# Twelve taps of a depthwise convolution move from the latents to behind the first eight softmax maxima and into the attention loop

## The chip, the cores and the metric

One core of a Trainium2 chip runs the whole program in one launch. The metric is the device time in microseconds (us). Before the change it is 3565.58 us, the median of three runs (3564.41 to 3566.22).

## The reference

Three transformer-like layers are computed one after the other on a sequence of 1024 positions and 1024 channels, in fp32. Only the second layer matters here. Cut to the part around the change:

```python
def hybrid_layer(h, ...):
    z = rms_norm(h, mix_norm_g) @ w_in
    a, gate, c_q, c_kv, k_r = jnp.split(z, ...)          # 512, 512, 384, 256, 32 columns
    u = a * jax.nn.sigmoid(gate)
    u = causal_depthwise_conv(u, conv_w, conv_b)         # 31 taps on 512 channels
    u = jax.nn.silu(layer_norm_2(u, conv_ln_g, conv_ln_b))
    q  = rms_norm(c_q, q_norm_g) @ w_uq                  # 8 heads of 64 + 32 (rotated)
    kv = rms_norm(c_kv, kv_norm_g) @ w_ukv
    ...
    o = block_causal_attention(qf, kf, v, chunk_id)      # softmax(q k) v, 8 heads
    mix = jnp.concatenate([rms_norm(u, conv_out_g), rms_norm(o, attn_out_g)], axis=-1)
    h = h + mix @ w_out
    ...
```

The convolution of u (31 taps, 4 blocks of 128 channels) does not depend on the attention, and the attention does not depend on it. Both must be there before the product with w_out.

## The kernel before, in words

The program is written out by hand, one list of instructions for each engine, with semaphores between them. Activations lie transposed: channels on the 128 partitions, the positions (1024, or 1044 with meta tokens and padding in layer 2) along the row. A product with weights is three matmuls, high part by high part and two cross terms (`product`, L253, its matmuls L270 to L272; `product_by_piece` L339 and `three` L320 with L324 to L326; `moving_product` L358 with L374 to L376). Weights come in tiles of eight 128x128 blocks: SyncE loads `w_raw`, ScalarE rounds it to `w_hi` (L131), GpSimd makes `w_lo` (L98 on POOL).

Layer 2's mixer is the class `Mixer2` (L1435). Its stages, in the order of the work:

- **The latents.** TensorE makes fourteen products from the input, each 8 blocks by 3 pieces of 348 columns: gate 0 and a 0, gate 1 and a 1, c 3, c 4, rot, then a sum over squares, c 0, c 1, c 2, another sum, gate 2, a 2, gate 3, a 3. A product takes three PSUM banks, and there are two such sets, so that each product waits until VectorE has read the last but one before it. VectorE reads them in `dve_gate` (L2088), `dve_row` (L2125), `dve_rotate_keys` (L2142) and `dve_normed` (L2137).
- **The heads' start.** Values (`pe_values`, L1693), the first keys and the first queries, which wait for five rows that VectorE writes to `x_lo` at the end of `dve`'s latents.
- **The first eight scores.** Before the attention loop TensorE computes the eight score tiles of head 0 (`pe_score`, L1741), and VectorE takes the maximum of each (`dve_max`, L2187, two TENSOR_REDUCE of line L113 each, and at some a small minimum), from which the softmax's shift comes. The score tiles lie in two places in PSUM, so that score n waits for the maximum n-2; the rows of shifts (`pe_row`, L1764) wait for the fifth and the eighth maximum, and the attention's first chunks wait for those rows.
- **The attention loop.** 160 slots, 20 for each of the 8 heads (`for c in range(len(CHUNKS2))`). In the slots 8 to 15 of a head the next head's eight scores and maxima are made in the same way, and in the slots before them its keys and queries.

The convolution is a side branch, a generator for each engine (`pe_branch`, `act_branch`, `dve_branch`, L1516 to L1616). The first 124 steps of VectorE's generator are the taps: one pass over a row of 1044 elements each, a TENSOR_SCALAR (L104) for the first tap of a block of channels and SCALAR_TENSOR_TENSOR (L107, `mix<-u_padded,vectors,mix`) for the other thirty. The layer norm of the result follows in 28 further steps, with sums on TensorE and squares, roots and the silu on ScalarE. `advance(branch, n)` issues n steps at that place of the engine's queue. A table of numbers says where:

```python
TAPS = dict(gate=[(0, 0), (1, 5), (1, 5), (1, 5)], a=(5, 5, 5, 0), row=(4, 5, 4, 5, 5), rot=2, kv=1, q=2)
STEPS, LAST_STEP = 91, 140
done = [min(x, self.LAST_STEP) * self.STEPS // self.LAST_STEP for x in (c, c + 1)]
```

`gate[c]` holds the taps before and after the second multiplication in `dve_gate`; `a[c]` those behind gate and product c; `row[i]` those behind row i (the rows go in the order 3, 4, 0, 1, 2); `rot`, `kv` and `q` those behind the rotation and the two normings. That is 61 in the latents. In the loop, slot c issues as many steps as its share of `STEPS` over 140 slots says (`taps`, L1511): 91 steps, of which 63 are the remaining taps. The generators of TensorE and ScalarE skip as many steps ahead of the loop (`early_taps`, L1506), so that the three stay in step.

Of the kernel before, what the change touches and what calls it, by code (L numbers as in the profile page):

```python
# [145 lines left out]
def advance(steps, n):  # L146

    for _ in range(n):
        if next(steps, None) is None:
            return  # L150


def drain(steps):
    for _ in steps:
        pass
# [10 lines left out]
def thirds_of(t):  # L166
    return t.rearrange("p (a b) -> p a b", a=3)
# [1267 lines left out]
class Mixer2:  # L1435
# [6 lines left out]

    TAPS = dict(gate=[(0, 0), (1, 5), (1, 5), (1, 5)], a=(5, 5, 5, 0), row=(4, 5, 4, 5, 5), rot=2, kv=1, q=2)
    ROUND_AT = 6
    SCORE_AT = {8: 3, 9: 8, 10: 2, 11: 7, 12: 1, 13: 6, 14: 4, 15: 5}
    ROW_AT = {15: (0,), 18: (1, 2)}
    SMALL = (0, 4, 8)
    STEPS, LAST_STEP = 91, 140  # L1450

    def __init__(self, core, ffn):
        self.k, self.ffn, s = core, ffn, core.s
# [51 lines left out]

    def early_taps(self):  # L1506

        return sum(sum(x) if isinstance(x, tuple) else x for x in (*self.TAPS["gate"], self.TAPS["a"], self.TAPS["row"], self.TAPS["rot"],
                                                                   self.TAPS["kv"], self.TAPS["q"]))

    def taps(self, c):  # L1511

# [575 lines left out]
    def dve_gate(self, v, c, branch):  # L2088
# [19 lines left out]
        else:  # L2108
            v.wait_ge(*p.done)
            v.settle()  # L2110
            v.tt(thirds_of(self.sig), k.view(p), thirds_of(self.rms), ALU.mult, inc=p)
        advance(branch, self.TAPS["gate"][c][0])
        v.wait_ge(self.gate_sig, c + 1)
        v.tt(self.sig, self.sig, self.rms, ALU.mult)
        advance(branch, self.TAPS["gate"][c][1])
        v.settle()
# [126 lines left out]
    def dve(self, v):  # L2243
        k = self.k
        branch = self.dve_branch(v)
        v.memset(self.u_pad[:, :, 0:CONV2 - 1], 0.0)
        for c in range(2):
            self.dve_gate(v, c, branch)
            advance(branch, self.TAPS["a"][c])
        for n, i in enumerate((3, 4)):  # L2250
            self.dve_row(v, i, n)
            advance(branch, self.TAPS["row"][i])
        self.dve_rotate_keys(v)
        advance(branch, self.TAPS["rot"])
        self.dve_normed(v, ("kv rms",), (3, 4), 2, "kv_norm_g_2")
        advance(branch, self.TAPS["kv"])
        for n, i in enumerate((0, 1, 2)):
            self.dve_row(v, i, n)
            advance(branch, self.TAPS["row"][i])
        self.dve_normed(v, ("q rms",), (0, 1, 2), 3, "q_norm_g_2")  # L2260
        advance(branch, self.TAPS["q"])
        for c in (2, 3):
            self.dve_gate(v, c, branch)
            advance(branch, self.TAPS["a"][c])
        for n, i in enumerate((3, 4, 0, 1, 2)):
            v.wait_ge(self.p_rounded, n + 1)
            v.tt(k.x_lo[:, i, :], self.T[i], k.x_hi[:, i, :].bitcast(F32), ALU.subtract, inc=self.p_ready)
        self.dve_heads(v)
        self.dve_at = [k.at["latents"][1]]
        self.dve_products(v, "heads")  # L2270
        for n in range(len(self.SCORE_AT)):
            self.dve_max(v, n)
        item = len(self.SCORE_AT)
        for c in range(len(CHUNKS2)):
            h, s = divmod(c, A_HEAD)
            self.dve_products(v, ("fill", c))
            if h + 1 < H2 and s in self.SCORE_AT:
                self.dve_max(v, item)
                item += 1
            advance(branch, self.taps(c))  # L2280
            if self.ended(c - 2) is not None:
                self.dve_inverse(v, self.ended(c - 2))
            if self.ended(c - 4) is not None:
                self.dve_head_out(v, self.ended(c - 4))
            if c >= self.LAST_STEP + 4 and c % 4 == 0:
                self.dve_u_row(v, (c - self.LAST_STEP) // 4 - 1)
        self.dve_inverse(v, 3 * H2 - 1)
        self.dve_head_out(v, 3 * H2 - 1)
        drain(branch)
        for c in range(4):  # L2290
            self.dve_o_row(v, c)
        for m in range(8):
            p, x = k.products["uo", m], k.res[:, m, :]
            v.wait_ge(*p.done)
            v.wait_ge(self.h0_back[m // 2], 48)
            v.tt(thirds_of(x), thirds_of(x), k.view(p), ALU.add, inc=p)
        self.dve_root(v, ("o rms",), self.A[0], self.A[1], 4, 4 * P)
        for m in range(8):
            p, x = k.products["oo", m], k.res[:, m, :]
            v.wait_ge(*p.done)  # L2300
            v.settle()
            v.tt(thirds_of(self.A[2]), k.view(p), thirds_of(self.A[0]), ALU.mult, inc=p)
            v.settle()
            v.tt(x, x, self.A[2], ALU.add, inc=self.added)
            v.wait_ge(self.h_square, m + 1)
            if m:
                v.settle()
                v.tt(self.T[8], self.T[8], self.T[9], ALU.add, inc=self.h_total)
            if m < 4:
                self.dve_out_row(v, m)  # L2310
        for m in range(4, 8):
            self.dve_out_row(v, m)
# [1171 lines left out]
```

## Time and profile before

| | before |
|---|---|
| median of 3 runs | 3565.58 us (3564.41 to 3566.22) |
| the profiled execution | 3567.81 us |
| its span on the core | 3565.7 us |
| mean granted TensorE clock | 0.978 |
| TensorE matmul busy | 3406.3 us (96%) |
| VectorE busy | 1775.1 us (50%) |
| ScalarE busy | 1118.9 us (31%) |
| GpSimd busy | 1085.4 us (30%) |
| stretch of the latents | about 1281 to 1445 us |
| first eight maxima | 1471.6 to 1481.1 us |
| attention loop | about 1482 to 1805 us |

In the rows below PE is TensorE, PEld its weight loads, DVE VectorE, ACT ScalarE, POOL GpSimd. A start is counted from the start of the span. What stands in square brackets behind an instruction is how long its engine sat idle before it, and whose instruction ended that; a short fall of the clock shows in the column PEclk, where 1.00 is the full level and 0.50 the half.

### The profile page before, as it was taken

What the parts mean: (1) busy time and instruction counts of PE and PEld (TensorE: products, weight loads), DVE (VectorE), ACT (ScalarE), POOL (GpSimd) and SP (SyncE); (2) the same over time, 40 slices, a digit from 0 to 9 for tenths busy, and PEclk for the clock granted to TensorE, in tenths of its full rate; (3) what the DMA queues carried; (4) which work ended last, traced back from release to release, by engine and by line L of the source; (5) the groups of instructions that cost most, each with busy time, mean ns of one, the idle gap of its engine ahead of it and who ended that gap; (6) DMA issues with size and microseconds to landing.
All of it is one profiled execution on the core that took longest, in us unless ns stands there. A gap on an engine that the chain in (4) does not pass through costs nothing.

```text
span 3565.7 us, 39250 instructions
## 1 busy us (share of the span) xinstructions
PE 3406.3 (96%) x16240; PEld 2787.2 (78%) x16240; DVE 1775.1 (50%) x1897; ACT 1118.9 (31%) x1493; POOL 1085.4 (30%) x1144
## 2 busy tenths in 40 slices
PE   8998899999999998899799999999999999999997
PEld 7665677888888688655489999999987788888776
DVE  4557553222223578777547546445475423444532
ACT  4333343111112432344533111111142523333442
POOL 3111344222333433100013434334334222222253
PEclk9999999999999999899899999999999999999998
DMA  3000221111111221000021111111112111010242
GB/s 126 24 24 24 101 71 60 53 48 48 48 48 49 76 84 40 26 7 7 6 76 45 42 54 42 48 49 47 48 42 107 54 65 53 30 36 31 82 142 95
DMA packets 56249, 192.21 MB, mean 54 GB/s; under 512 B 6900, under 2 KB 7284, under 8 KB 55560
## 3 DMA queue, kind: packets, MB, share of 16 engines
q1 hardware_dynamic: 56072, 189.71, 15.4%
q8 instruction: 128, 2.10, 0.2%
q14 instruction: 49, 0.40, 0.0%
HBM read 172.83 MB, written 16.86 MB: 53 GB/s over the span
## 4 chain that ended last, share of the span: by engine, by line
PE 80%; DVE 14%; ACT 4%; issue 1%; DMA 0%; POOL 0%; DVEq 0%; ACTq 0%; SPq 0%; POOLq 0%
PE psum L270 21%; PE psum L271 21%; PE psum L272 21%; PE psum L138 11%; DVE mix L107 3%; DVE work L98 3%; PE psum L324 2%; PE psum L326 2%; PE psum L325 2%; DVE res L98 1%; DVE res L107 1%; DVE softmax_shift_columns L113 1%; DVE u_padded L98 1%; PE psum L136 1%; DVE work L116 1%
## 5 line engine op out<-in xcount | busy, mean ns | idle before, releaser
L98 POOL TENSOR_TENSOR w_lo<-w_raw,w_hi 128x256 fp32r<-128x256 f32 x1140 | 1085.2, 983 | 2445.6 <-ACT w_hi L131 2445.6
L270 PE MATMUL psum<-x_hi,w_hi 128*128 128x512 f32 (+2 forms) x3240 | 1202.9, 371 | 12.6 <-DVE mix L98 5.9
L271 PE MATMUL psum<-x_lo,w_hi 128*128 128x512 f32 (+2 forms) x3240 | 1165.8, 360 | 0.0
L272 PE MATMUL psum<-x_hi,w_lo 128*128 128x512 f32 (+2 forms) x3240 | 1161.9, 359 | 0.0
L131 ACT CAST w_hi<-w_raw 128x1024 fp32r<-128x1024 f32 x285 | 298.2, 1048 | 1503.7 <-PE psum L272 1429.7
L270 PEld LDWEIGHTS psum<-x_hi,w_hi 128*128 128x128 f32 x3240 | 613.5, 189 | 101.7 <-issue 18.6
L271 PEld LDWEIGHTS psum<-x_lo,w_hi 128*128 128x128 f32 x3240 | 613.0, 189 | 82.9 <-issue 18.4
L272 PEld LDWEIGHTS psum<-x_hi,w_lo 128*128 128x128 f32 x3240 | 611.2, 189 | 70.2
L270 PE MATMUL psum<-h_hi,w_hi 128*128 128x512 f32 x824 | 325.2, 395 | 3.1 <-DVE res L98 3.1
L272 PE MATMUL psum<-h_hi,w_lo 128*128 128x512 f32 x824 | 320.8, 389 | 0.0
L271 PE MATMUL psum<-h_lo,w_hi 128*128 128x512 f32 x824 | 320.7, 389 | 0.0
L107 DVE SCALAR_TENSOR_TENSOR res<-res,psum 128x1024 f32<-128x1024 f32 (+1 forms) x88 | 90.3, 1026 | 238.6 <-PE psum L272 229.3
L270 PEld LDWEIGHTS psum<-h_hi,w_hi 128*128 128x128 f32 x824 | 154.7, 188 | 37.8 <-DVE res L98 3.5
L271 PEld LDWEIGHTS psum<-h_lo,w_hi 128*128 128x128 f32 x824 | 154.7, 188 | 34.2 <-issue 2.6
L272 PEld LDWEIGHTS psum<-h_hi,w_lo 128*128 128x128 f32 x824 | 154.6, 188 | 32.3
L138 PE MATMUL psum<-res 128*65 128x256 f32 (+5 forms) x480 | 172.7, 445 | 7.1 <-ACT res L131 4.2
L98 DVE TENSOR_TENSOR h_tmp<-h_tmp 128x1024 f32<-128x1024 f32 (+1 forms) x36 | 54.7, 1518 | 240.7 <-ACT h_tmp L126 240.7
L107 DVE SCALAR_TENSOR_TENSOR mix<-u_padded,vectors,mix 128x1044 f32<-128x1044 f32 x120 | 168.5, 1404 | 5.0 <-ACT work L131 0.8
L98 DVE TENSOR_TENSOR up<-psum,ffn_rms 128x1026 f32<-128x1026 f32 x44 | 54.0, 1226 | 191.1 <-PE psum L272 189.4
L324 PE MATMUL psum<-x_hi,w_hi 128*128 128x348 f32 (+2 forms) x328 | 130.1, 397 | 18.2 <-DVE x_lo L98 9.2
L107 DVE SCALAR_TENSOR_TENSOR up_conv<-up,vectors,up_conv 128x1024 f32<-128x1024 f32 x88 | 143.7, 1633 | 3.1
L98 DVE TENSOR_TENSOR res<-res,psum 128x1024 f32<-128x1024 f32 (+1 forms) x56 | 68.5, 1224 | 140.9 <-PE psum L272 135.8
(281 smaller groups left out, 3730.5 us busy)
## 6 DMA issues: line engine op xcount, KB each, us to landing
w_raw<-w_dram SPq DMA_DIRECT2D x285, 512.0 KB, 3.2
res<-spill SPq DMA_DIRECT2D x4, 1044.0 KB, 8.9
res<-x_dram SPq DMA_DIRECT2D x8, 512.0 KB, 9.0
res<-x_dram SPq DMA_DIRECT2D x4, 1024.0 KB, 8.1
spill<-res SPq DMA_DIRECT2D x1, 4096.0 KB, 13.8
spill_a<-mix SPq DMA_DIRECT2D x8, 512.0 KB, 2.9
res<-spill_a SPq DMA_DIRECT2D x8, 512.0 KB, 4.7
x_plain<-spill SPq DMA_DIRECT2D x4, 1024.0 KB, 9.4
```

The costliest lines, as they stand in the source:

```text
L98: self.mark(self.e.tensor_tensor(out, a, b, op), inc)
L107: self.mark(self.e.scalar_tensor_tensor(out, a, s, b, op0, op1), inc)
L113: self.mark(self.e.tensor_reduce(out, a, AX.X, op, negate=negate), inc)
L116: self.mark(self.e.reciprocal(out, a), inc)
L131: self.mark(self.e.copy(out, a), inc)
L138: ins = self.e.matmul(out, lhsT, rhs, start=start, stop=stop, skip_group_check=True)
L270: t.e.matmul(out, whi, xhi, start=k == 0, stop=False, skip_group_check=True)
L271: t.e.matmul(out, whi, xlo, start=False, stop=False, skip_group_check=True)
L272: ins = t.e.matmul(out, wlo, xhi, start=False, stop=last_k, skip_group_check=True)
L324: t.e.matmul(out, whi, xhi, start=first, stop=False, skip_group_check=True)
L325: t.e.matmul(out, whi, xlo, start=False, stop=False, skip_group_check=True)
L326: return t.e.matmul(out, wlo, xhi, start=False, stop=last, skip_group_check=True)
```

## The change

Twelve taps leave the latents: five behind row 4 (the taps just ahead of the rotation), three behind row 2, four behind gate and product 2. Eight of them go one behind each of the first eight maxima, ahead of the loop. The other four go to the loop, whose `STEPS` rise from 91 to 95. `early_taps` counts the eight, so that the other engines' generators start the loop at step 57 and not 61; the last step stays in slot 139.

```diff
-    TAPS = dict(gate=[(0, 0), (1, 5), (1, 5), (1, 5)], a=(5, 5, 5, 0), row=(4, 5, 4, 5, 5), rot=2, kv=1, q=2)
+    TAPS = dict(gate=[(0, 0), (1, 5), (1, 5), (1, 5)], a=(5, 5, 1, 0), row=(4, 5, 1, 5, 0), rot=2, kv=1, q=2)
...
-    STEPS, LAST_STEP = 91, 140
+    STEPS, LAST_STEP = 95, 140
...
     def early_taps(self):

-        return sum(sum(x) if isinstance(x, tuple) else x for x in (*self.TAPS["gate"], self.TAPS["a"], self.TAPS["row"], self.TAPS["rot"],
-                                                                   self.TAPS["kv"], self.TAPS["q"]))
+        return len(self.SCORE_AT) + sum(sum(x) if isinstance(x, tuple) else x for x in (
+            *self.TAPS["gate"], self.TAPS["a"], self.TAPS["row"], self.TAPS["rot"], self.TAPS["kv"], self.TAPS["q"]))
...
         for n in range(len(self.SCORE_AT)):
             self.dve_max(v, n)
+            advance(branch, 1)
```

By the table, the taps of each head's 20 slots (slots 0 to 7, 8 to 14, 15 to 19) were 5, 4 and 4 in every head, 13 in all. Now heads 0, 2 and 4 have 5, 5 and 3 (still four of them in slots 9 to 14, and one in slot 8), and heads 1 and 3 have 6, 4 and 4: in head 1 the slots 5, 6 and 7 have a tap each, where two of them had one, and in head 3 slot 0 has the added one. The last tap of all moves from slot 16 of head 4 to slot 18, and the steps of the layer norm behind it come one or two slots later, up to head 6.

VectorE's queue in the latents, behind row 4 of the products (`work<-work` adds the squares; `mix<-psum,mix` and `psum<-psum,mix` are the first two instructions of the rotation of the keys, which reads the product rot):

```order
 L98 TENSOR_TENSOR res<-psum,work 128x1044
 L98 TENSOR_TENSOR work<-work 128x1044
-L107 SCALAR_TENSOR_TENSOR mix<-u_padded,vectors,mix 128x1044 x5
 L98 TENSOR_TENSOR mix<-psum,mix 32x1044
 L98 TENSOR_TENSOR psum<-psum,mix 32x3x348
```

The five taps between row 4 and the rotation are gone; nothing else moved there.

VectorE's queue at the first maxima, before (each pair of TENSOR_REDUCE is one maximum):

```order
L98 TENSOR_TENSOR work<-work 32x348
L113 TENSOR_REDUCE softmax_shift_columns<-psum 128x1
L113 TENSOR_REDUCE own_chunk_shift<-psum 64x1
L113 TENSOR_REDUCE softmax_shift_columns<-psum 128x1
L113 TENSOR_REDUCE own_chunk_shift<-psum 64x1
L113 TENSOR_REDUCE softmax_shift_columns<-psum 128x1
L113 TENSOR_REDUCE own_chunk_shift<-psum 64x1
```

and now:

```order
L98 TENSOR_TENSOR work<-work 32x348
L113 TENSOR_REDUCE softmax_shift_columns<-psum 128x1
L113 TENSOR_REDUCE own_chunk_shift<-psum 64x1
L107 SCALAR_TENSOR_TENSOR mix<-u_padded,vectors,mix 128x1044
L113 TENSOR_REDUCE softmax_shift_columns<-psum 128x1
L113 TENSOR_REDUCE own_chunk_shift<-psum 64x1
L107 SCALAR_TENSOR_TENSOR mix<-u_padded,vectors,mix 128x1044
L113 TENSOR_REDUCE softmax_shift_columns<-psum 128x1
L113 TENSOR_REDUCE own_chunk_shift<-psum 64x1
L107 SCALAR_TENSOR_TENSOR mix<-u_padded,vectors,mix 128x1044
```

One tap stands behind every maximum, up to the eighth.

VectorE's queue at the end of the latents (`u_padded<-psum,work` ends product 2 and product 3 of a; the first `work<-psum,work` reads gate 3):

```order
 L98 TENSOR_TENSOR u_padded<-psum,work 128x1044
-L107 SCALAR_TENSOR_TENSOR mix<-u_padded,vectors,mix 128x1044 x5
+L107 SCALAR_TENSOR_TENSOR mix<-u_padded,vectors,mix 128x1044
 L98 TENSOR_TENSOR work<-psum,work 128x1044
 L107 SCALAR_TENSOR_TENSOR mix<-u_padded,vectors,mix 128x1044
```

Four of the five taps ahead of gate 3 are gone.

## Rows read from the trace of the kernel before

**Rows 1.** The page: the chain that ended last, shares by engine.

```profile
PE 80%; DVE 14%; ACT 4%; issue 1%; DMA 0%; POOL 0%; DVEq 0%; ACTq 0%; SPq 0%; POOLq 0%
```

**Rows 2.** Waits of PE in the latents and heads' start: us in total, times, longest.

```profile
PE psum L270 <- DVE mix L98: 5.3, 1, 5.3
PE psum L374 <- DVE x_lo L98: 3.9, 1, 3.9
...
PE psum L270 <- DVE work L98: 2.4, 1, 2.4
```

**Rows 3.** Timeline of DVE behind row 4: start, us, instruction, xcount, idle before.

```profile
1338.64 7.17 DVE L107 SCALAR_TENSOR_TENSOR mix<-u_padded,vectors,mix 128x1044 f32<-128x1044 f32 x5
1345.94 1.25 DVE L98 TENSOR_TENSOR mix<-psum,mix 32x1044 f32<-32x1044 f32 x1
```

**Rows 4.** Timelines of ACT and PE: the end of rot, the start of c 0.

```profile
1342.79 1.05 ACT L131 CAST w_hi<-w_raw 128x1024 fp32r<-128x1024 f32 x1 [5.46 <-PE psum L272]
...
1349.81 0.66 PE L270 MATMUL psum<-x_hi,w_hi 128*128 128x348 f32 x1 [5.35 <-DVE mix L98]
```

**Rows 5.** Windows: us, busy (x) of PE, PEld, DVE, ACT, POOL; PEclk, DMA share, GB/s.

```profile
1306.70:1312.00 5.30, 5.27 (x23) 5.28 (x24) 5.22 (x4) 2.02 (x2) 3.14 (x3) 0.68 0.27 99
...
1349.80:1355.00 5.20, 5.20 (x18) 5.20 (x19) 5.03 (x4) 0.00 (x0) 0.00 (x0) 0.50 0.11 44
1355.00:1361.00 6.00, 6.00 (x39) 6.00 (x38) 5.83 (x7) 0.00 (x0) 0.00 (x0) 1.00 0.00 0
```

**Rows 6.** Timeline of DVE: start of the norming of q, behind row 2.

```profile
1399.35 1.25 DVE L98 TENSOR_TENSOR work<-squares 128x1044 f32<-128x1044 f32 x1 [2.84 <-ACT squares L126]
```

**Rows 7.** Timelines of DVE and ACT at the end of the latents.

```profile
1430.62 1.25 DVE L98 TENSOR_TENSOR work<-psum,work 128x1044 f32<-128x1044 f32 x1
1443.17 7.08 DVE L98 TENSOR_TENSOR x_lo<-res,x_hi 128x1044 fp32r<-128x1044 f32 x5
...
1429.44 1.05 ACT L131 CAST w_hi<-w_raw 128x1024 fp32r<-128x1024 f32 x1 [10.35 <-PE psum L272]
1441.80 4.91 ACT L131 CAST x_hi<-res 128x1044 fp32r<-128x1044 f32 x5
```

**Rows 8.** The chain that ended last, in order of time, at the first maxima.

```profile
1473.94 1.14 PE psum L138 x2
...
1481.17 4.57 PE psum L138 x11
```

**Rows 9.** Timeline of DVE at the first maxima and behind them.

```profile
1471.61 0.51 DVE L113 TENSOR_REDUCE softmax_shift_columns<-psum 128x1 fp32r<-128x336 f32 x1 [1.95 <-PE psum L138]
...
1475.10 1.04 DVE L113 TENSOR_REDUCE softmax_shift_columns<-psum 128x1 fp32r<-128x848 f32 x1 [0.56 <-PE psum L138]
...
1477.52 0.91 DVE L113 TENSOR_REDUCE softmax_shift_columns<-psum 128x1 fp32r<-128x720 f32 x1 [0.15 <-PE psum L138]
...
1480.96 0.16 DVE L98 TENSOR_TENSOR softmax_shift_columns<-softmax_shift_columns 128x2 fp32r<-128x2 f32 x1
1488.35 0.52 DVE L98 TENSOR_TENSOR work<-psum,mix 64x348 f32<-64x348 f32 x1 [7.23 <-PE psum L326]
```

**Rows 10.** Windows of the first maxima and of the loop's start, columns as in rows 5.

```profile
1471.00:1482.00 11.00, 7.65 (x25) 4.71 (x26) 8.14 (x20) 0.79 (x2) 0.00 (x0) 0.50 0.00 0
1482.00:1502.00 20.00, 19.56 (x71) 11.48 (x70) 10.49 (x14) 9.70 (x24) 5.27 (x4) 0.85 0.02 3
```

**Rows 11.** Taps by tile (duration ns min/median/max), and POOL's one group on the page.

```profile
L107 DVE SCALAR_TENSOR_TENSOR mix<-u_padded,vectors,mix x120: 1304/1306/1807, 1298.6 to 1670.2; 128x1044 f32<-128x1044 f32 x120
...
L98 POOL TENSOR_TENSOR w_lo<-w_raw,w_hi 128x256 fp32r<-128x256 f32 x1140 | 1085.2, 983 | 2445.6 <-ACT w_hi L131 2445.6
```

**Rows 12.** Timeline of DVE in the attention loop: next head's second maximum, slack behind the eighth.

```profile
1544.23 1.16 DVE L113 TENSOR_REDUCE softmax_shift_columns<-psum 128x1 fp32r<-128x960 f32 x1 [0.90 <-PE psum L138]
...
1684.80 0.52 DVE L98 TENSOR_TENSOR work<-psum,mix 64x348 f32<-64x348 f32 x1 [5.94 <-PE psum L326]
1699.83 1.25 DVE L98 TENSOR_TENSOR u_padded<-u_padded 128x1044 f32<-128x1044 f32 x1 [1.14 <-ACT u_padded L126]
```

## The prediction, made before the change was run

> **What bounds the kernel now.** The page's chain comes first: TensorE holds 80% of the path, VectorE 14% [rows 1]. So a moved VectorE instruction costs or saves only where TensorE waits for VectorE. The second view is the list of TensorE's waits in the latents and up to the first scores [rows 2]. The reader should see three waits for VectorE: 5.3 us of L270, the first matmul of product c 0; 3.9 us of L374, the first of the values; and 2.4 us of L270 at product c 3, where no tap moves, but which shows what a shorter wait does to the clock. The third view is the timeline around each place that loses or gains taps [rows 3, 4, 6, 7], the fourth the chain and the timeline at the first eight maxima [rows 8, 9]. There the chain alternates: a score on TensorE, its maximum on VectorE, the score that reuses its place, and behind the last maximum TensorE starts 4.57 us of the chain's work. Only that stretch has neither a product nor an older chunk for TensorE to do meanwhile.
>
> A tap in a stretch without GpSimd's work takes 1.31 us, the least and the median of 120 [rows 11]; with some 0.03 us to the next one's start I count **1.34 us** for each.
>
> **Part 1: five taps behind row 4.** They run from 1338.64 for 7.17 us; the rotation starts at 1345.94 [rows 3], and TensorE's c 0 at 1349.81, after 5.35 us idle [rows 4]. Without them the rotation is not free at 1338.6: it reads the product rot, whose end releases ScalarE's cast at 1342.79 [rows 4]. So it starts at about 1342.8, 3.1 us earlier, and c 0 as well: **-3.1 us**. Late next is rot itself; the norming of kv and row 0 follow 3.1 us earlier too. TensorE's idle time shrinks to about 2.2 us, and that touches the clock. Behind the idle 5.35 us the granted clock is at the half level (1.2 GHz): 18 matmuls in 5.20 us, where at the full level 39 take 6.00 us [rows 5], so 18 would take 2.8 us, and 2.4 us are lost. But behind the idle 2.4 us ahead of c 3 [rows 2] the clock fell as well: 23 matmuls in 5.30 us instead of 3.5 us, 1.8 us lost [rows 5]. The clock's share of the gain lies between 0 (still falls, as long as now) and 2.4 us. I take **-1.1 us**, near the middle, as the idle time that will be left is nearest to the 2.4 us that still cost 1.8 us.
>
> **Part 2: three taps behind row 2.** Nothing. VectorE's next instruction, the norming of q, already waits 2.84 us for ScalarE's root [rows 6]; it would wait 6.9 us.
>
> **Part 3: four taps behind a 2.** VectorE reads gate 3 at 1430.62 right behind the last tap, though the product was done by 1429.44 [rows 7]: 1.2 us of four taps' 5.4 come back, the rest turns into waiting. By the end that is less still: the first x_lo at 1443.17 needs the rounded row that ScalarE begins at 1441.80 and has by about 1442.8 [rows 7]. **-0.4 us.** The latents thus give 4.6 us, between 3.5 and 5.9.
>
> **Part 4: eight taps behind the maxima.** The eight maxima run from 1471.61 to 1481.12 [rows 9], 9.5 us, with 8.14 us busy [rows 10]. VectorE waited for a score only 0.56 and 0.15 us in it [rows 9]. Seven taps come ahead of the eighth maximum: 7 x 1.34 = 9.4 us, less the 0.7 us of those waits, since a score has its matmuls done (1.14 us in the chain, [rows 8]) while two taps and the small maximum between them run. The eighth tap falls into the 7.23 us in which VectorE waits behind the maxima [rows 9]; it costs nothing, and if that gap went, 1.34 us. Nothing of the rest is hidden: queued behind each tap is the next maximum, for that waits the score two further on, for the eighth the rows of shifts, for these the first chunks; and TensorE's queue is in order, so keys and queries of head 1 stand behind them. Then it is busy 19.56 of 20.00 us [rows 10], and makes up for nothing. **+8.7 us**, bounds 8.0 and 9.4. The clock is at the half level throughout this stretch already [rows 10]. It comes back somewhere in the 20 us behind it, where the mean is 0.85, that is 6 us at the half level, 3 us lost; that can become up to 1.8 us less or more, by where the first busy work falls. I take 0.
>
> **Part 5: four taps more in the loop.** Two of the four come behind the last maximum of head 4's slots, ahead of a 5.94 us wait of VectorE [rows 12]: nothing. Head 3's comes in slot 0, at the corresponding wait: nothing. Head 1's comes just ahead of the next head's first maximum, where the second maximum waits 0.90 us for its score [rows 12]: 1.34 - 0.90 = **+0.4 us**. Bounds: 0, and 4 x 1.34 = 5.4 us if none is covered. GpSimd's instructions meet some of these taps. The longest tap took 1.807 us, 0.5 us over the median [rows 11]. The Trainium skill (SBUF — State Buffer, section Who interferes with whom) says that of a VectorE instruction with two SBUF inputs and a GpSimd one that reads SBUF the second fully blocks until the first is done; a tap could then take 1.31 + 0.98 = 2.29 us, and four of them would make the sum up to 3.8 us larger. The trace has no such tap among 120, and the sum goes by it.
>
> **Part 6: the norm of u one or two slots later.** One of its steps, a subtraction with a wait of 1.14 us for ScalarE's square and a sum [rows 12], slips from ahead of the first maximum of its head to between the second and the third. TensorE waits for VectorE at both places. 0, between -2 and +3.7 us (1.14 and two rows of 1.25 us, all in series).
>
> **The sum:** -3.1 - 1.1 - 0.4 + 8.7 + 0.4 = **+4.5 us**. On the profiled execution (3567.81 us, span 3565.7 us) that is 3572.3 us; it lies 2.2 us above the median of the runs, 3565.58 us, so that I predict 3565.6 + 4.5 = **3570.1 us**. 0.2%, about what a measurement of this kernel can tell from no change, is 7.1 us: the likeliest outcome is slower by less than that.
>
> **The rivals.**
> - *The taps of the loop are not covered.* Place: slots 5 to 15 of heads 0 to 4, where taps stand between maxima and TensorE waits for them. If each of the four costs its 1.34 us, the sum is +9.5 us: 3575.1 us. It decides from three of them on, where the sum passes 7.1 us. For it: the chain runs through such taps already. Against it: the table leaves four in slots 9 to 14 of each head, as before.
> - *The norm's step lands in the maxima chain.* +3.7 us in head 5, in all +8.2 us: 3573.8 us. Against it: at that head VectorE was the late one before the first maximum already, so that the step only changes its place.
> - *The latents give nothing back*, since each product has its own next wait and the clock falls all the same: +9.1 us, 3574.7 us. Against it: rot's end and the start of its reader lie 3.1 us apart [rows 3, 4].
> - *The maxima are not on the path*, as when scores or rows of shifts run further ahead than the chain says: -4.6 + 0.4 = -4.2 us, 3561.4 us. For it: TensorE is busy 7.65 of the 11 us [rows 10]. Against it: the chain [rows 8].
> - That the change does not do what it says is out by the order of the queues: the taps stand behind the maxima.
>
> **How the numbers follow.** The forecast has 0.66; its own range is 3566.6 to 3572.6 us, from -5.9 + 8.7 - 1.8 to -3.5 + 8.7 + 1.8 us. Uncovered loop taps have 0.13, the norm's step 0.06, latents without gain 0.05, free maxima 0.08, something not seen 0.02. Slower by over 0.2% is the second to the fourth: 0.24. Within 0.2% are the forecast and the free maxima, less 0.01 for a case that gains more: 0.73. Faster by over 0.2%: 0.03. The range starts below the forecast's own one, at 3563.5 us (1.2 us of spread between runs and 1.8 us of clock), leaves out the free maxima, and ends at 3577.0 us, above uncovered taps with another 1.8 us of clock.
>
> **What would show it.** In the changed kernel's profile: the 5.3 us wait of L270 is near 2.2 us, the rotation starts right behind rot; the norming of q waits some 6.9 us; from the first to the eighth maximum 18.2 us, with VectorE busy nearly all of it and no wait for a score; in the chain taps (L107) between the maxima. The loop from its first chunk to the last slot is as long as now within 2 us. I am wrong if the maxima take clearly less than 17 us, if the latents shorten by more than 6 us, or if the loop moves by more than 3 us either way.

## The result and the profile after

| | before | after |
|---|---|---|
| median of 4 runs | 3565.9 us (3564.41 to 3567.03) | 3584.31 us (3581.2 to 3587.31) |
| ratio | | 1.005 (1.0038 to 1.0062) |
| the profiled execution, its span | 3567.81 us, 3565.7 us | 3585.78 us, 3583.7 us |
| mean granted TensorE clock | 0.978 | 0.976 |
| VectorE busy | 1775.1 us | 1777.3 us |

The change costs 18.4 us. 4.5 us were forecast, and the time lies outside the range. One execution of a kernel further down (the subtractions of the mean alone) took 4181.94 us at a granted clock of 0.838, where its other ten have 0.976 to 0.978, and its ratio is taken without it.

The chain's shares on the page, as [rows 1]:

```profile
PE 82%; DVE 12%; ACT 4%; issue 1%; DMA 0%; POOL 0%; DVEq 0%; ACTq 0%; SPq 0%; POOLq 0%
```

VectorE's share fell and TensorE's rose. That says little about the loss: the fastest kernel below (all four moved out of heads 0 and 2), 10 us faster than before, has the same 82% and 12%. The place of the loss has to be read from single waits.

The latents and the eight maxima did what was forecast. TensorE's waits there, in the changed kernel (as [rows 2]: us in total, times, longest):

```profile
PE psum L374 <- DVE x_lo L98: 3.9, 1, 3.9
...
PE psum L270 <- DVE work L98: 2.4, 1, 2.4
PE psum L270 <- DVE mix L98: 2.2, 1, 2.2
```

5.3 us have become 2.2 us. The timelines of VectorE and of TensorE, same kernel (start, us, instruction, xcount, idle time before it):

```profile
1335.82 1.25 DVE L98 TENSOR_TENSOR work<-work 128x1044 f32<-128x1044 f32 x1 [1.14 <-ACT work L126]
1341.25 1.25 DVE L98 TENSOR_TENSOR mix<-psum,mix 32x1044 f32<-32x1044 f32 x1 [4.19 <-PE psum L272]
...
1393.86 1.25 DVE L98 TENSOR_TENSOR work<-squares 128x1044 f32<-128x1044 f32 x1 [7.21 <-ACT squares L126]
...
1466.36 0.51 DVE L113 TENSOR_REDUCE softmax_shift_columns<-psum 128x1 fp32r<-128x336 f32 x1 [1.89 <-PE psum L138]
...
1467.16 1.31 DVE L107 SCALAR_TENSOR_TENSOR mix<-u_padded,vectors,mix 128x1044 f32<-128x1044 f32 x1
1468.50 1.16 DVE L113 TENSOR_REDUCE softmax_shift_columns<-psum 128x1 fp32r<-128x960 f32 x1
...
1482.94 0.77 DVE L113 TENSOR_REDUCE softmax_shift_columns<-psum 128x1 fp32r<-128x592 f32 x1
...
1484.40 1.31 DVE L107 SCALAR_TENSOR_TENSOR mix<-u_padded,vectors,mix 128x1044 f32<-128x1044 f32 x1
1490.89 0.52 DVE L98 TENSOR_TENSOR work<-psum,mix 64x348 f32<-64x348 f32 x1 [5.19 <-PE psum L326]
```

```profile
1345.12 0.43 PE L270 MATMUL psum<-x_hi,w_hi 128*128 128x348 f32 x1 [2.21 <-DVE mix L98]
```

The rotation starts right behind rot; the norming of q waits 7.21 us where it waited 2.84 [rows 6]; no maximum waits for a score any more; the eighth tap shortens VectorE's gap behind the maxima from 7.23 us [rows 9] to 5.19 us. The windows of the same kernel, columns as in [rows 5]:

```profile
1345.10:1350.30 5.20, 5.18 (x23) 5.18 (x24) 5.03 (x4) 2.02 (x2) 0.11 (x1) 0.67 0.31 101
...
1466.00:1485.00 19.00, 7.57 (x24) 4.23 (x23) 17.79 (x28) 0.55 (x2) 0.00 (x0) 0.50 0.00 0
1485.00:1505.00 20.00, 19.56 (x76) 11.16 (x74) 11.77 (x15) 9.94 (x24) 5.79 (x4) 0.88 0.01 2
```

Behind the shorter wait the clock is 0.67 where it was 0.50 [rows 5].

**Where the rest comes from.** The table takes the layer apart at marks that are found in each trace: `work<-work` behind row 4 (1337.36 us in the kernel before), the first maximum (the `128x336` one), the eighth (`128x592`), then the first maximum in each head's slots (slot 8 of head 0 to 6), and at last the last `u_padded<-psum,u_padded`, behind the product with w_out (1901.39). The first row is the kernel before in us, the others the difference from it; the labels follow the order of the experiments below. All are from one profiled execution each, and free of what differs ahead of the layer. "0-1" is from head 0's slots to head 1's.

| kernel | latents | maxima | to loop | 0-1 | 1-2 | 2-3 | 3-4 | 4-5 | 5-6 | tail | sum |
|---|---|---|---|---|---|---|---|---|---|---|---|
| before, us | 134.25 | 8.08 | 23.04 | 39.84 | 35.86 | 39.17 | 35.87 | 48.23 | 53.40 | 146.29 | 564.03 |
| the change | -3.7 | +8.5 | -0.6 | +3.0 | -0.8 | +2.1 | +4.4 | -1.7 | +6.0 | +2.1 | +19.3 |
| e1_loop_as_before | -3.9 | +8.5 | -0.7 | 0 | 0 | 0 | 0 | 0 | +1.1 | +1.5 | +6.4 |
| e2_loop_only | 0 | 0 | +0.1 | +3.0 | -0.9 | +0.6 | +1.2 | -0.1 | +8.6 | +1.1 | +13.7 |
| e3_norm_later | -4.0 | +8.5 | -0.6 | -0.5 | +2.8 | +1.5 | 0 | -1.8 | +4.5 | +2.0 | +12.4 |
| e4_taps_moved | -3.9 | +8.5 | -0.5 | +3.0 | -0.9 | +2.1 | +4.4 | +0.8 | -0.1 | -0.1 | +13.4 |
| e5_covered | -3.8 | +8.5 | -0.5 | -0.5 | 0 | 0 | 0 | 0 | -0.1 | -0.1 | +3.5 |
| e6_ahead_of_head_out | 0 | 0 | 0 | +3.0 | 0 | +2.9 | 0 | +1.3 | -0.1 | -0.1 | +7.0 |
| e7_silu_later | -0.1 | 0 | 0 | 0 | 0 | 0 | 0 | 0 | +2.6 | +0.3 | +2.9 |
| e8_behind_last_maximum | -3.9 | 0 | +0.1 | 0 | 0 | 0 | 0 | 0 | 0 | 0 | -3.8 |
| e9_even_heads | -0.3 | 0 | 0 | -2.5 | 0 | -2.5 | 0 | +1.6 | -0.1 | 0 | -3.8 |
| e10_both | -3.7 | 0 | +1.8 | +0.5 | 0 | -2.6 | 0 | +1.1 | +1.3 | +1.6 | 0 |
| e11_centre_later | -0.1 | 0 | 0 | 0 | 0 | 0 | 0 | -1.3 | +4.9 | -0.1 | +3.4 |
| e12_all_moved | -3.9 | 0 | +0.1 | -4.2 | 0 | -3.6 | 0 | +1.3 | -0.1 | -0.1 | -10.5 |

Up to the loop the change has +4.2 us (-3.7, +8.5, -0.6), as forecast. The other 15 us come in the loop and behind it. Most of them can be read at two kinds of places.

**A tap ahead of a head's output.** In head 0, VectorE before and after, one fence each:

```profile
1515.49 0.62 DVE L113 TENSOR_REDUCE softmax_shift_columns<-psum 128x1 fp32r<-128x448 f32 x1
1516.14 0.23 DVE L113 TENSOR_REDUCE own_chunk_shift<-psum 64x1 f32<-64x64 f32 x1
1516.40 0.55 DVE L98 TENSOR_TENSOR mix<-res,psum 64x384 f32<-64x384 f32 x1
```

```profile
1516.93 0.62 DVE L113 TENSOR_REDUCE softmax_shift_columns<-psum 128x1 fp32r<-128x448 f32 x1
1517.58 0.23 DVE L113 TENSOR_REDUCE own_chunk_shift<-psum 64x1 f32<-64x64 f32 x1
1517.85 1.31 DVE L107 SCALAR_TENSOR_TENSOR mix<-u_padded,vectors,mix 128x1044 f32<-128x1044 f32 x1
1519.18 0.55 DVE L98 TENSOR_TENSOR mix<-res,psum 64x384 f32<-64x384 f32 x1
```

The tap that stood in slot 15 of heads 0, 2 and 4, behind the last maximum, stands in slot 14 now, and slot 14 ends with the copy of a finished part of the head's output, which frees the bank that TensorE's next products of probabilities need. TensorE's timeline, before and after:

```profile
1517.00 0.70 PE L138 MATMUL psum<-work,x_plain 97*128 97x256 f32 x2 [1.57 <-DVE mix L98]
```

```profile
1519.78 0.70 PE L138 MATMUL psum<-work,x_plain 97*128 97x256 f32 x2 [2.81 <-DVE mix L98]
```

1.2 us more of waiting; and behind it the clock falls. The windows behind the two waits, before and after:

```profile
1517.00:1520.40 3.40, 3.40 (x18) 1.93 (x19) 3.23 (x6) 1.53 (x6) 0.00 (x0) 1.00 0.00 0
```

```profile
1520.20:1523.60 3.40, 3.40 (x10) 1.29 (x8) 3.23 (x6) 0.76 (x4) 0.00 (x0) 0.55 0.00 0
```

10 matmuls in 3.4 us where 18 fitted: about 1.5 us. With the wait that makes 2.7 of the +3.0 us of 0-1. Head 2 has the same at slot 14: TensorE's wait grows from 1.56 to 2.32 us.

The +4.4 us of 3-4 come at another copy of the kind. In head 4 the tap that stood in slot 4 stands in slot 3 now, ahead of the copy `mix<-res,psum 64x256`; two taps in a row stand there where there was one, and TensorE waits 1.31 us for that copy, where the kernel before has no wait over 0.3 us there. The rows are in the last section. No run moved this tap alone, so that its part is read from the traces only.

**The norm's steps.** In head 5 the subtraction of the mean that stood ahead of the first maximum, with the sum of squares that waits for ScalarE, stands between the second and the third. In head 6 ScalarE's silu comes one slot later. ScalarE before, and after (both at the turn from head 5 to 6):

```profile
1731.27 1.28 ACT L126 ACT_TABLE_LOAD   x1
1732.56 4.70 ACT L126 ACTIVATE mix<-mix,vectors 128x1044 f32<-128x1044 f32 x4
1737.28 1.28 ACT L126 ACT_TABLE_LOAD   x1
1738.58 0.48 ACT L126 ACTIVATE res<-psum 16x384 f32<-16x384 f32 x1
```

```profile
1747.64 0.48 ACT L126 ACTIVATE res<-psum 16x384 f32<-16x384 f32 x1 [1.31 <-PE psum L138]
...
1750.74 1.28 ACT L126 ACT_TABLE_LOAD   x1
1752.03 4.70 ACT L126 ACTIVATE mix<-mix,vectors 128x1044 f32<-128x1044 f32 x4
1756.75 1.28 ACT L126 ACT_TABLE_LOAD   x1
```

and TensorE before and after:

```profile
1739.11 0.91 PE L138 MATMUL psum<-work,x_plain 97*128 97x384 f32 x2 [3.43 <-ACT res L126]
1742.25 1.54 PE L138 MATMUL psum<-res 16*65 16x384 f32 x2 [2.23 <-ACT res L131]
```

```profile
1717.30 3.85 PE L138 MATMUL psum<-u_padded,ones 128*128 128x348 f32 x6 [2.48 <-DVE u_padded L98]
...
1760.07 1.54 PE L138 MATMUL psum<-res 16*65 16x384 f32 x2 [8.66 <-ACT res L131]
```

ScalarE is in the silu and its two table loads (ACT_TABLE_LOAD, a change of its function table) for 7.3 us; waits of 3.43 and 2.23 us became one of 8.66. The wait of 2.48 us between head 5's maxima is the sum's; it was not there before.

### The profile page after: what moved, and what is told of

It is laid out like the page before. It is cut to its first block, busy times and chain, and to the rows that moved or that the text cites. A ratio compares the mean times of both kernels' runs of the same rounds, so it can differ in the third digit from the quotient of the medians.

```text
span 3583.7 us, 39250 instructions
## 1 busy us (share of the span) xinstructions
PE 3410.0 (95%) x16240; PEld 2787.0 (78%) x16240; DVE 1777.3 (50%) x1897; ACT 1119.2 (31%) x1493; POOL 1086.9 (30%) x1144
## 4 chain that ended last, share of the span: by engine, by line
PE 82%; DVE 12%; ACT 4%; issue 1%; DMA 0%; POOL 0%; DVEq 0%; ACTq 0%; SPq 0%; POOLq 0%
PE psum L270 22%; PE psum L271 22%; PE psum L272 22%; PE psum L138 10%; DVE mix L107 2%; DVE work L98 2%; PE psum L324 2%; PE psum L326 2%; PE psum L325 2%; DVE res L98 1%; DVE softmax_shift_columns L113 1%; PE psum L136 1%; DVE work L116 1%; DVE res L107 1%; DVE u_padded L98 1%
## 6 DMA issues: line engine op xcount, KB each, us to landing
x_plain<-spill SPq DMA_DIRECT2D x4, 1024.0 KB, 10.5
```

## The experiments

All change one thing of the kernel before or of the change; the loop's table is the function `taps`, where `x` counts slots (head h begins at 20 h) and `steps(x)` is the number of steps done ahead of slot x; where a diff shows only a line of `steps`, `done` in `taps` is taken from it:

```diff
-        done = [min(x, self.LAST_STEP) * self.STEPS // self.LAST_STEP for x in (c, c + 1)]
+        done = [self.steps(min(x, self.LAST_STEP)) for x in (c, c + 1)]
```

Medians are of 6, 7 or 11 executions, and are given against those of the kernel before in the same series (18 to 33 executions).

**The loop left alone** (to the change):

```diff
-    TAPS = dict(..., a=(5, 5, 1, 0), row=(4, 5, 1, 5, 0), ...)
-    STEPS, LAST_STEP = 95, 140
+    TAPS = dict(..., a=(5, 5, 5, 0), row=(4, 5, 1, 5, 0), ...)
+    STEPS, LAST_STEP = 91, 140
```

> The change with the loop over the slots left alone: eight taps behind the maxima, taken from behind rows 4 (five) and 2 (three); the four behind a 2 stay, and the loop has its 91 steps at their old slots. Theory A (the time is lost in the loop, by its table of 95): only the maxima's +8.5 us and the latents' -4.2 us are left, so about +4.3 us, 3570 us, and the first maximum of each head stays 3 to 6 us behind that of the kernel before. Theory B (the loop only passes on what the eight maxima did, as by a later start of loads or another state of the buffers): as the whole change, +18 us, 3584 us.

3573.71 us against 3567.58, ratio 1.0018 (1.0009 to 1.0028). Two thirds of the loss are gone, and by the table all five stretches up to head 5 are as before to 0.1 us. The loop doesn't pass on what the maxima did. The +1.1 and +1.5 us in 5-6 and the tail are the clock's: the order there is word for word that of the kernel before, TensorE's idle time is the same within 0.3 us, and the granted clock is 0.78 against 0.81 in the one stretch and 0.95 against 0.97 in the other.

**The loop alone** (to the kernel before):

```diff
-    TAPS = dict(..., a=(5, 5, 5, 0), ...)
-    STEPS, LAST_STEP = 91, 140
+    TAPS = dict(..., a=(5, 5, 1, 0), ...)
+    STEPS, LAST_STEP = 95, 140
```

> The kernel before with one thing changed: four taps go from behind a 2 to the loop, whose table has 95 steps; rows 2 and 4 keep their taps, nothing stands behind the maxima. Theory A: the loop's loss alone, +13 to +14 us less 0.4 us of the latents, about 3579 us. Theory B: nothing is lost without the maxima, 3566 us within 2 us.

3578.82 us against 3567.58, ratio 1.0029 (1.0018 to 1.0041): four taps that went from a place without cost to the loop, with the slide of the whole table, cost 11 us alone. This and the 6.1 us of the run with the loop left alone make 17.4 of the 18.4 us.

**Norm later, and taps moved** (to the change, two kernels):

```diff
+    # norm later
+        if x <= 96:
+            return x * 91 // 140 + sum(x > 20 * h + 17 for h in range(3))
+        return x * 95 // 140
...
+    # taps moved
+        return x * 95 // 140 if x <= 96 else x * 91 // 140 + 4
```

> The change, with the taps of heads 0 to 4 at the old slots, three of the added ones in slots 17 of heads 0 to 2, and from slot 96 (head 4, slot 16) on the table of 95: so the last taps and every step of the norm of u stand where the change has them, one or two slots late. Theory A1 (the norm's steps cost it: the sum and the subtractions between maxima, and ScalarE's sigmoid-linear step with two table loads ahead of a copy that TensorE waits for): +4 us of latents and maxima, and about +6.5 us from head 5 on, 3576 to 3577 us. Theory A2 (the places of the taps in heads 0 to 4 cost it, by late releases and the clock that falls after them): nothing from head 5 on, 3570 us.

> The counterpart: taps up to slot 95 as the change has them, from there on the old slots, with two taps in slot 96 (head 4, slot 16); the norm's steps stand as in the kernel before. Theory A2: +4 us and the +8.6 us by which heads 1 to 4 fell behind, 3578 us. Theory A1: only the +4 us of latents and maxima, 3570 us. If both cost, this run and the one with the norm later share the 14 us between them, some 8 and 6 us.

3578.96 and 3578.14 us against 3567.58, ratios 1.0033 (1.0022 to 1.0045) and 1.003 (1.0019 to 1.0042). Both cost: over the run with the loop left alone, 5.3 and 4.4 us by the medians, together 9.7 of the 12.3 us that the whole change has over it (the difference is within what these medians can tell). By the table the taps of the one cost 9.4 us in heads 0 to 4, and the norm's steps of the other 2.7 us net in 4-5 and 5-6, where 1.8 us come back first. The run with the later norm had a surprise: the stretches behind its added taps in slot 17 of heads 1 and 2 cost 2.8 and 1.5 us, though these taps stand behind the last maximum. VectorE and TensorE in head 1, kernel with the norm later:

```profile
1564.57 0.52 DVE L98 TENSOR_TENSOR work<-psum,mix 64x348 f32<-64x348 f32 x1
```

```profile
1565.70 0.49 PE L324 MATMUL psum<-x_hi,w_hi 128*128 128x348 f32 x1 [1.98 <-DVE work L98]
```

Behind its run of five taps in head 1 VectorE reads a product that was long ready, and TensorE waits 1.98 us for VectorE's result, against 0.48 us with four taps. In head 0 the same run is followed by gaps of VectorE. So "behind the maxima" is not enough; it must be in front of a gap. Head 2's +1.5 us is no cost of its tap: TensorE is idle as long as before in that stretch (3.9 us), and only the granted clock differs, 0.96 against 1.00; the next run has two added taps in the same slot at no cost.

**Added taps in slots 17 of heads 0 and 2** (to the change):

```diff
+        return x * 91 // 140 + 2 * (x > 17) + 2 * (x > 57)
```

> The change with the loop's four added taps in slots 17 of heads 0 and 2, two in each, all else of the loop at its old slots. There VectorE waits for the next head's products after its run of taps (0.9 and 6.0 us in head 0 of the kernel before), while the same place in head 1 has no such gap, and a tap put there in the run with the later norm made TensorE's wait 1.5 us longer. Theory A (the loop loses by the places of single steps, each ahead of something that TensorE waits for): the four cost nothing, and the time is that of the run with the loop left alone, 3570 to 3574 us, 8 us or more under the whole change. Theory C (the number of taps in the loop is what costs, VectorE being full): 4 x 1.34 us and the clock on top, 3578 us or more.

3571.76 us against 3567.74, ratio 1.0011 (1.0003 to 1.002). VectorE in head 0:

```profile
1520.43 9.36 DVE L107 SCALAR_TENSOR_TENSOR mix<-u_padded,vectors,mix 128x1044 f32<-128x1044 f32 x7
1529.82 0.17 DVE L116 RECIPROCAL softmax_inverse_columns<-psum 128x2 f32<-128x2 f32 x1
1534.12 0.52 DVE L98 TENSOR_TENSOR work<-psum,mix 64x348 f32<-64x348 f32 x1 [4.13 <-PE psum L326]
```

Seven taps in a row, and still 4.13 us of waiting behind them: the four added taps are free here, and the number of taps in the loop is not what costs. This kernel moves the same twelve taps as the change, and is 4.0 us slower than before where the change is 18.4 us slower; that is nearly the difference that the prediction gave the change, 4.5 us. The steps of the norm, too, stand at their old slots in it.

**One tap ahead of the head's output** (to the kernel before):

```diff
+        return x * 91 // 140 + (x in (15, 55))
```

> The kernel before with the tap of slot 15 made in slot 14, in heads 0 and 2: nothing is added, two taps only stand ahead of the copy of a head's output (mix<-res,psum 64x384), which frees the bank that TensorE waits for. Theory A: TensorE's wait for that copy grows from 1.6 to 2.8 us at each, and the granted clock falls to the half level behind it: +2 to +3 us for each, 3571 to 3573 us against 3567 us. Theory C: nothing, 3567 us.

3575.23 us against 3567.74, ratio 1.0019 (1.0011 to 1.0028). TensorE in head 0, and the window behind:

```profile
1515.13 0.78 PE L138 MATMUL psum<-work,x_plain 97*128 97x256 f32 x2 [2.90 <-DVE mix L98]
```

```profile
1515.30:1518.70 3.40, 3.40 (x10) 1.61 (x10) 3.23 (x6) 0.76 (x4) 0.00 (x0) 0.55 0.00 0
```

Nearly the same wait (2.90 against 2.81 us) and the same fall of the clock as in the change, +3.0 and +2.9 us for two taps that moved by one slot. Nothing was added.

**The silu alone one slot later** (to the kernel before):

```diff
+        return x * 91 // 140 - (x == 122)
```

> The kernel before with one step of the norm of u one slot later, ScalarE's four sigmoid-linear activations with their table loads in slot 2 of head 6 in place of slot 1; VectorE's and TensorE's order is untouched. Theory A1: ScalarE is then in this step for 7.3 us while TensorE has run out of work, so its waits of 3.4 and 2.2 us become one of some 8.7 us: +3 us, 3570 us. Theory A1 wrong: the step is as late as before for everyone, 3567 us within 1 us.

3572.82 us against 3567.74, ratio 1.0014 (1.0005 to 1.0023). TensorE's one wait there:

```profile
1743.51 1.54 PE L138 MATMUL psum<-res 16*65 16x384 f32 x2 [8.66 <-ACT res L131]
```

8.66 us, as in the change; 5.1 us by the medians, 2.9 us by the trace, whose run (3571.70 us) was below its median.

**Row 4's five taps behind the eighth maximum** (to the kernel before):

```diff
-    TAPS = dict(..., row=(4, 5, 4, 5, 5), ...)
+    TAPS = dict(..., row=(4, 5, 4, 5, 0), ...)
...
         for n in range(len(self.SCORE_AT)):
             self.dve_max(v, n)
+        advance(branch, 5)
```

> The kernel before with one thing changed: the five taps behind row 4 go behind the eighth maximum, all five, where VectorE waits 7.23 us for the next product; the loop is untouched. By the steps of the prediction: -3.1 us by c 0 and 0 to -1.8 us by the clock, five taps of 6.7 us fit into the gap: 3562.5 to 3564 us, if the kernel before runs at 3567 us. If the latents' gain doesn't reach the end, or the first rows of shifts and their chunks need VectorE in that gap: 3567 us or more.

3568.43 us against 3567.74, ratio 0.9998 (0.9989 to 1.0007), the runs from 3560.74 to 3569.84: can't be told from no change. Its trace has the -3.8 us up to the end of the layer, and its run gave 2.8 us back behind it: over the 102 us from TensorE's first wait for a sum there, the granted clock was 0.95 where the kernel before has 0.98. Whether that goes with the edit or with the run stays open.

**The taps of slots 12 and 13 moved out** (two kernels: to the kernel before, and to the one with row 4's taps moved):

```diff
+        return x * 91 // 140 - sum((x > 20 * h + 12) + (x > 20 * h + 13) - 2 * (x > 20 * h + 17) for h in (0, 2, 4))
```

> The kernel before with the taps of slots 12 and 13 of heads 0, 2 and 4 made in slot 17 of the same head, behind the maxima; nothing added, nothing else moved. If single places decide (theory A), the reverse of what the change did must gain: TensorE's waits of 0.7 us for the reciprocals and 1.6 us for the copy of the head's output go, and no wait comes in slot 17 of an even head: about -2.2 us for each head, -4.5 to -7 us in all, 3561 to 3563 us against 3567.7 us. If VectorE's load as a whole decides (theory C), or TensorE next waits for something else as long: 3567 us.

> The run before and the five taps of row 4 behind the eighth maximum together. Theory A: the two lie at different places and add up, -3.8 us (the loop of that run began so much earlier by its trace) and what the even heads give: 3557 to 3560 us. If the gain of the latents is lost again behind the loop, as its median of -0.7 us may say: no faster than the even heads alone.

3566.20 us and 3563.46 us against 3568.28, ratios 0.9995 (0.9987 to 1.0004) and 0.9985 (0.9976 to 0.9994). Heads 0 and 2 give 2.5 us each. In head 4 the same move ends at +1.6 us in 4-5, of which 1.3 us also show up in two kernels with no edit there; it gains nothing. The first can't be told from no change, the second is 0.15% faster; in its profiled run 1.8 us were lost between the eighth maximum and head 0's slots, and 0-1 ended at +0.5 us where the first has -2.5 us, with a granted clock of 0.92 there against 1.00 in the kernel before.

**The subtractions of the mean alone** (to the kernel before):

```diff
+        return x * 91 // 140 - (103 < x < 110)
```

> The kernel before with the four subtractions of the mean (and the sums of squares behind them) in head 5 one to two slots later, in slots 4, 6, 7 and 9 as the change has them, the last with its sum between the second and the third maximum; the sums before and the sigmoid-linear step after them stay. Theory A1: +4 to +5 us between head 5's first and eighth maximum, 3572 us. The prediction's bound for it was +3.7 us, its value 0: 3567.7 us.

3572.35 us against 3568.28, ratio 1.001 (1.0001 to 1.002): +4.9 us in head 5's stretch, less 1.3 us in the one ahead. TensorE and VectorE:

```profile
1706.18 3.77 PE L138 MATMUL psum<-u_padded,ones 128*128 128x348 f32 x6 [4.46 <-DVE u_padded L98]
```

```profile
1704.88 1.25 DVE L98 TENSOR_TENSOR u_padded<-u_padded 128x1044 f32<-128x1044 f32 x1 [1.14 <-ACT u_padded L126]
...
1711.05 1.04 DVE L113 TENSOR_REDUCE softmax_shift_columns<-psum 128x1 fp32r<-128x848 f32 x1 [4.26 <-PE psum L138]
```

TensorE stands at the norm's sum, and VectorE waits 4.26 us for the scores queued behind it. In this kernel the sum kept its old slot; in the change it comes one slot later, behind more work, and its wait is 2.48 us. The loss is as large even so: from head 5's first to its eighth maximum the kernel before takes 18.33 us, this one 23.36 us and the change 23.48 us.

**All four moved out of heads 0 and 2** (with row 4's taps behind the eighth maximum):

```diff
+        return x * 91 // 140 - sum((x > 20 * h + 9) + (x > 20 * h + 10) + (x > 20 * h + 12) + (x > 20 * h + 13)
+                                   - 2 * (x > 20 * h + 17) - 2 * (x > 20 * h + 22) for h in (0, 2))
```

> Row 4's five taps behind the eighth maximum, and in heads 0 and 2 all four taps that stand between maxima (slots 9, 10, 12, 13) moved: two to slot 17 and two to slot 2 of the next head, into the 6.0 us in which VectorE waits for the next head's product. Theory A: also the 0.8 us that TensorE waits in the maxima goes, so -3 us for each of the two heads and -3.8 us of the latents: 3557 to 3559 us, if the clock falls no more often than before. If two taps in slot 2 delay the rotation that TensorE's values wait for: above the run with both.

3558.16 us against 3568.28, ratio 0.9973 (0.9962 to 0.9984): 10 us faster than the kernel before. The trace has -10.5 us, of which the latents give 3.9 and the two heads 4.2 and 3.6 us. VectorE in head 0:

```profile
1506.36 9.36 DVE L107 SCALAR_TENSOR_TENSOR mix<-u_padded,vectors,mix 128x1044 f32<-128x1044 f32 x7
1515.75 0.17 DVE L116 RECIPROCAL softmax_inverse_columns<-psum 128x2 f32<-128x2 f32 x1
1515.96 2.65 DVE L107 SCALAR_TENSOR_TENSOR mix<-u_padded,vectors,mix 128x1044 f32<-128x1044 f32 x2
1520.23 0.52 DVE L98 TENSOR_TENSOR work<-psum,mix 64x348 f32<-64x348 f32 x1 [1.63 <-PE psum L326]
```

All of it fits ahead of the product that VectorE waits for anyway; of the gap of 5.98 us in the kernel before 1.63 us are left.

## Why the prediction was wrong, step by step

- **Part 1, right.** -3.1 us for c 0: 1349.81 to 1345.12, with the layer's start 1.54 us earlier, is 3.15 us. The wait fell to 2.21 us as forecast, and the clock behind it rose from 0.50 to 0.67. **Part 2, right**: q waits 7.21 us (6.9 forecast). **Part 3, -0.4 us forecast, measured 0**: the run with the loop alone takes these four taps away, and its latents are as long as before. The latents gave 3.7 us, within the 3.5 to 5.9 of the text but below its 4.6.
- **Part 4, right.** The eight maxima take +8.5 us (+8.7 forecast). They were the only thing that I had expected to cost much, and they are less than half of the loss.
- **Part 5, wrong, and the step that failed.** It priced "four taps more in the loop" at +0.4 us and asked only where the four *added* taps fall, and took the others as staying. With 95 steps for 91 the whole table slides: at slot 14 of heads 0, 2 and 4, and at slot 3 of head 4, a tap moved over the one line that matters, from behind to ahead of a copy of the head's output. The text looked straight at this ("four in slots 9 to 14 of each head, as before", as its argument against the rival of uncovered taps) and counted, where it should have asked what stands behind each in its slot. Measured: +8.7 us from 0-1 to 3-4 by the trace, above the bound of 5.4 us, which had only the taps' own time in it. The clock was left out: one tap of 1.3 us ahead of a wait costs 3.0 us. That the places cost this, and not the number of taps, is shown by the run that moved two taps by one slot (7.5 us slower by the medians) and by the one that added four in front of gaps at no cost. The rival "not covered" had the place, and with 3575.1 us half the price.
- **Part 6, wrong.** It priced one step of VectorE, between -2 and +3.7 us, and took 0. That step measures +4.9 us less 1.3 us in the run with the subtractions alone, where TensorE's sum waits for it with the scores queued behind. ScalarE's silu, which moves as well, was not priced at all: +2.6 us by its own trace, +5.1 us by its medians. The two do not simply add up in the change: from head 5's eighth maximum to head 6's first it takes 0.8 us more than before, where the run with the silu alone takes 2.6 us more; what gives the rest back was not looked for. The argument that VectorE was the late one already, "so that the step only changes its place", held for VectorE and not for TensorE's queue.
- **What the sum would have been.** The prediction's own sign of being wrong was a loop that moves by more than 3 us; it moved by 13.0 us. With the measured terms: -3.7 + 8.5 - 0.6 up to the loop, +8.7 us for the stretches 0-1 to 3-4, +4.3 us for 4-5 and 5-6, +2.1 us in the tail, 19.3 us in all, and 17.8 us with the layer's earlier start; the profiled executions differ by 18.0 us. The tail's 2.1 us are not settled. They are not the clock's alone: the granted clock over the tail is 0.97, as before (the 1.5 us of the run with the loop left alone come at 0.95). The two other kernels with all of the norm's steps later have +1.1 and +2.0 us there, the two with one of its steps moved 0.3 and -0.1, so that it may be the later steps of the norm in head 6; no run moved them alone.

## What to carry to other kernels

A table that spreads work over slots by a ratio moves every entry when its total changes: compare the order before and after slot by slot on all engines, and ask of each entry that crossed a line what stands behind it in its own queue and who waits for that. Price a step that delays a nearly always busy TensorE by its own time and by the clock that may fall behind it, together here up to three times the step. Put spare work in front of a gap of the engine that does it, and only there: the same twelve taps cost 18.4 us or 4.0 us by the places of four of them and of the steps that slid with them, and moving row 4's five taps and eight of those between maxima in front of gaps gave 10 us. Row 4's five alone gave nothing that the medians can tell.

## What was not expected of the hardware

The same wait has two prices. At slot 3 of head 4 VectorE's order is the same in the change and in the kernel with the loop alone, two taps ahead of the output copy, and so is TensorE's wait for it. The change, then the loop alone:

```profile
1657.06 0.50 PE L136 MATMUL psum<-identity,res 1*128 1x1 f32 x4 [1.31 <-DVE mix L98]
```

```profile
1650.05 0.36 PE L136 MATMUL psum<-identity,res 1*128 1x1 f32 x4 [1.30 <-DVE mix L98]
```

and the windows behind the two waits:

```profile
1656.90:1663.90 7.00, 6.84 (x18) 3.48 (x19) 3.63 (x6) 1.92 (x5) 2.03 (x2) 0.51 0.22 75
```

```profile
1650.00:1657.00 7.00, 6.95 (x32) 3.95 (x32) 5.80 (x9) 2.52 (x8) 1.92 (x2) 1.00 0.23 77
```

With 1.31 us of idle time the clock fell to the half level and 18 matmuls ran in 7 us; with 1.30 us it stayed, and 32 ran. The stretch 3-4 cost 4.4 us in the one and 1.2 us in the other, and all of that comes late in it: from head 3's first maximum to VectorE's first `work<-psum,mix` of head 4 the two kernels and the one before take 21.0 us each. The kernel with the taps moved has the wait as 1.30 us too, and there the clock fell and the stretch cost 4.4 us, so that the hundredth of a microsecond is not what decides. The Trainium skill (TensorE: Matmul & The Clock Gate, section What's actually happening) says that the same kernel shows more or fewer matmuls at the low clock by the phase at which it starts; the rows fit that, and do not show the cause by themselves. So a forecast for such a wait is a range, here 1.2 to 4.4 us, and one profiled run can lie 5 us off the median of its kernel, as that of the kernel with row 4's taps and the even heads' moved together (3568.42 against 3563.46 us).

A switch of ScalarE's table cost its load here and no more: the load begins at 1731.27 and takes 1.28 us, and the activation starts at 1732.56. The Trainium skill (ScalarE: Activation LUTs, section What ACT_TABLE_LOAD costs) gives the same duration for the load and about as much again for a drain; here the trace disagrees, since 0.01 us lie between the end of the load and the next activation, and 0.02 us between the last activation and the load back (1737.28).
